# Expert weights as plain fp32 matmuls on column tiles, with two neighbouring down rows in each partition

## The chip, the cores and the metric

The kernel runs on one core of one Trainium2 chip, as one launch. A core has TensorE (PE in the profile, with the weight loads as PEld), VectorE (DVE), ScalarE (ACT), GpSimd (POOL) and SyncE (SP), which here only issues transfers, and 16 DMA engines. The metric is device time in microseconds (us). A "unit" below is 128 partitions x 2048 fp32 elements of weights, 1 MB.

## The reference, cut to what matters

Two pre-norm layers run on 256 tokens of width 1024 in fp32. Each begins with a mixer (a gated recurrence and a windowed attention side by side, merged and projected by w_o). Layer 0 has a dense SwiGLU, layer 1 has experts: each token goes to the two best of eight SwiGLU experts of inner width 3584.

```python
def moe_swiglu(h, w_router, wg, wu, wd):
    logits = (t @ w_router).astype(jnp.float32)
    top_vals, top_idx = lax.top_k(logits, TOP_K)          # TOP_K = 2 of 8
    w = jax.nn.softmax(top_vals, axis=-1)
    gates = jnp.sum(jax.nn.one_hot(top_idx, N_EXPERTS, ...) * w[..., None], axis=1)
    def expert(acc, xs):
        g_e, wg_e, wu_e, wd_e = xs                        # 1024x3584, 1024x3584, 3584x1024
        return acc + g_e[:, None] * swiglu(t, wg_e, wu_e, wd_e), None
...
for i in range(DEPTH):
    ...
    x = x + (swiglu(...) if i % 2 == 0 else moe_swiglu(h2, ...))
    gate_p = jax.nn.sigmoid(rms_norm(x, g_ple[i]) @ w_ple_gate[i])
    x = x + gate_p * (p[i] @ w_ple_up[i])
```

The last two lines are the "PLE" step; it follows the experts in layer 1 and ends the program. With the inputs of this case the router sends 69, 55, 61, 67, 62, 69, 65 and 64 tokens to experts 0 to 7.

## The kernel before

**Where the weights go.** Every weight of the program passes as units through one DMA queue, that of SP, into six `raw` slots (`load_unit`, L459). ACT copies a unit from `raw` into `w_hi`, rounded to the matmul type fp32r (L626). DVE subtracts that copy from `raw` into `w_lo`, the remainder (L984). Both have three slots. PE then makes three fp32r products for each tile of the unit: high x high and high x low of the activations (`high_products`, L1637 and L1638; in other stages L1629 and L1631), and low x high (L1644; L1630). A `raw` slot is free again, and SP may load the next unit into it, when DVE has made its `w_lo` (`low_ready`). `w_hi` and `w_lo` slots are free when PE has used the unit (`units_used`).

**The experts.** They run as items, one for each expert and up to five extra ones when an expert has more than `ROWS` = 88 tokens. Each item multiplies its 88 gathered rows (88 columns of `hT`) with one expert's weights in seven steps of 512 inner columns: two gate units, two up units, two down units each, so 42 units an item and 336 in all for eight items. One matmul of an item has 128 x 88 on one side and 512 columns of weights on the other. In a step, ACT makes the silu of the gate, DVE multiplies it with the up product, PE transposes that in four 128-column pieces (`flip`, L2103), and ACT and DVE split the result into high and low for the down product. POOL gathers the next item's rows from DRAM (`x_slots<-x_rows`, L589) and adds the finished item's rows into `x_sum` in DRAM (L583), both as indirect DMAs. The router, its `place` in each expert's list, and the first item's gather by a selection matrix stand ahead of item 0, together with the products of the PLE up projection (`ple_up_tile`). The mixer's last weights are those of w_o, whose products have the lines L1652 to L1654.

**The end.** The last item's rows are not stored but spread over the tokens by a selection matrix (`spread_piece`). DVE adds the result to x (`add_last`, L1535), PE transposes x, ACT and DVE make high and low parts of it, and then come four PLE gate units (L1629 to L1631), the sigmoid, and the output.

**What sets the order.** Each engine has its own program, written out by hand; the loops over items are `Fori` loops on every engine. Loads are issued in the order in which units are used, as slots come free.

Of the kernel before, what the change touches and what calls it, by code (L numbers as in the profile page):

```python
# [53 lines left out]
ROWS = 88  # L54
# [6 lines left out]
def build_trunk(nc, x_in, p_in, lb_logits, g_mix, w_in, q_norm, k_norm, sinks, hgrn_norm, w_pa, w_pb, w_o,  # L61
# [14 lines left out]
    EXTRA = 5  # L76
    ITEMS = EXPERTS + EXTRA + 1
    assert DEPTH == 2 and TILES == 2 and D == 1024 and HW == BANK and SW == BANK and D_FF % BANK == 0
    assert PLE == 2 * P and SEQ <= 3 * ROWS and 2 * TOP_K * SEQ < (EXTRA + 1) * (2 * ROWS + 1) and KV * 2 == 256
# [15 lines left out]
    PER_ITEM = STEPS * PER_STEP  # L95
    assert PER_ITEM % SLOTS == 0 and PER_ITEM % RAW_SLOTS == 0

# [43 lines left out]
    MOE = UP1 + 1  # L141
    MIX_AT = [MIX0, MIX1]
    END = MOE + GATE_UNITS
# [10 lines left out]
    STAGE_OF_NORM = [None, WO0_OUT, DENSE_OUT, PLE0_OUT, WO1_OUT]  # L154
    P_BANK = [4, 7]
# [9 lines left out]
    def item_down(s):  # L165
        return item_up(s + 1) + G_UNITS if s + 1 < STEPS else PER_ITEM - D_UNITS

    with ExitStack() as ctx:
# [6 lines left out]
        raw = sb("raw", [P, RAW_SLOTS, UNIT])  # L175
        w_hi = sb("w_hi", [P, SLOTS, UNIT], F32R)
        w_lo = sb("w_lo", [P, SLOTS, UNIT], F32R)
        x = sb("x", [P, TILES, D])
# [12 lines left out]
        x_slots = wide[:, 1024:2048]  # L191
        gain_rows = wide[:, 2048:3072]
        y_rows = wide[:, 3072:4096]
# [5 lines left out]
        spread = [innerT[0][:, t, P:2 * P] for t in range(TILES)]  # L199
        last_y = [[a[:, 4 * half:4 * half + 4, P:2 * P] for half in range(2)] for a in hT]  # L200
        deep = arena[:, 7680:12800]
        x_gained = deep[:, 3072:5120].rearrange("p (t n) -> p t n", t=TILES)
# [14 lines left out]
        pick = qk_mem[:, 0:256].rearrange("p (t s) -> p t s", t=TILES)  # L217
# [39 lines left out]
        logit_parts = qk_mem[0:2 * EXPERTS, 2 * SEQ:3 * SEQ]  # L257
        add_parts = sb("add_parts", [2 * EXPERTS, EXPERTS])
        pairs_mem = score_mem[:, 0:2 * TILES * EXPERTS * EXPERTS].rearrange("p (n t e f) -> p n t e f", n=2, t=TILES, e=EXPERTS)
# [10 lines left out]
        extra_of = sb("extra_of", [P, EXTRA, EXPERTS])  # L270
        second_of = sb("second_of", [P, EXTRA, EXPERTS])
        slot_columns = sb("slot_columns", [P, TILES, 2])
# [6 lines left out]
        slot_now = sb("slot_now", [P, 3])  # L279
        slot_next = sb("slot_next", [P, 3])  # L280
        slot_token = sb("slot_token", [P, 1], I32)
        sum_token = sb("sum_token", [P, 1], I32)
        pad_row = sb("pad_row", [P, 1])
        pad_now = sb("pad_now", [P, 1])
        pool_spare = sb("pool_spare", [P, 1])
        extra_expert = sb("extra_expert", [P, EXTRA])
# [12 lines left out]

        def last_act(a, part):  # L300
            return a[:, 2 * part:2 * part + 2, :].rearrange("p k (t c) -> p k t c", t=TILES)
# [9 lines left out]
        p_loaded = sem("p_loaded")  # L311
        raw_filled = [sem(f"raw{s}_filled") for s in range(RAW_SLOTS)]
# [25 lines left out]
        counted = sem("counted")  # L338
        gates_ready = sem("gates_ready")
        rows_stored = sem("rows_stored")  # L340
        slots_done = sem("slots_done")
# [5 lines left out]
        tokens_ready = sem("tokens_ready")  # L347
        spare_written = sem("spare_written")
        slot_copied = sem("slot_copied")
        slots_loaded = sem("slots_loaded")  # L350
# [57 lines left out]
        picks_ready = sem("picks_ready")  # L408
        gathered = sem("gathered")
        gatheredT_high = sem("gatheredT_high")  # L410
        gatheredT_ready = sem("gatheredT_ready")
        spread_ready = sem("spread_ready")
        slot_next_ready = sem("slot_next_ready")
        item_silu = sem("item_silu")
        item_act = sem("item_act")
        item_act_transposed = sem("item_act_transposed")
        item_actT_high = sem("item_actT_high")
        item_actT = sem("item_actT")
        item_y_done = sem("item_y_done")
        item_y_ready = sem("item_y_ready")  # L420
        last_y_high = sem("last_y_high")
        last_y_low = sem("last_y_low")
# [1813 lines left out]
```

## Time and profile before

| | |
|---|---|
| median of 3 runs | 1620.01 us (1619.46 to 1621.54) |
| profiled execution, its span | 1622.3 us |
| PE busy | 1606.5 us, 99% |
| DVE busy | 1272.1 us, 78% |
| ACT busy | 1082.4 us, 67% |
| bytes moved | 477.66 MB, mean 294 GB/s |
| the 40 slices of 40.6 us | 131 to 332 GB/s in the first 16, about 350 to 394 GB/s in the rest |

The profiled execution's only time is its span, 2.3 us above the median of the runs. Of the span, the mixers, the dense stage and layer 0's PLE fill the first 630 us, the eight items lie between about 646 and 1592 us, and the rest is the last PLE step. "Busy" of PE counts matmuls with their modelled ends, so 99% says that a matmul was nearly always in flight. A DMA share of 1 means that each of the 16 engines had a packet at all times. PEclk is the clock granted to TensorE as a share of 2.4 GHz.

### The profile page before, as it was taken

How to read it: one execution, taken by the hardware profiler on the slowest of the kernel's cores; microseconds unless marked ns; L12 is line 12 of the kernel's file. 1: busy time of each engine (PE TensorE's matmuls, PEld its weight loads, DVE VectorE, ACT ScalarE, POOL GpSimd, SP SyncE). 2: the span in 40 equal slices, each digit the busy share in tenths (PEclk: the TensorE clock that was granted, in tenths of full speed). 3: DMA queues.
4: the chain of work that ended last, by engine and by line, in shares of the span. 5: the costliest groups of instructions: out<-in, count | busy, mean ns of one | idle time of the engine just before them, and what ended most of it. 6: DMA issues, size and time to landing. Idle time of an engine off the chain costs nothing.

```text
span 1622.3 us, 22022 instructions
## 1 busy us (share of the span) xinstructions
PE 1606.5 (99%) x8472; PEld 1326.4 (82%) x8472; DVE 1272.1 (78%) x1065; ACT 1082.4 (67%) x910; POOL 103.1 (6%) x82
## 2 busy tenths in 40 slices
PE   9999999999999999999999999999999999999998
PEld 7888888888887887888888888888888888888886
DVE  7876655444578667998888888988888888889886
ACT  6665543443556656877778778778778778777774
POOL 0100000000001001050010010010010010010010
PEclk9999999999999999999999999999999999999999
DMA  9444565555464345999999999999999999999992
GB/s 332 171 157 156 185 204 181 182 197 192 159 195 148 131 156 177 393 376 379 389 380 384 393 350 388 390 377 383 389 355 386 394 363 385 386 382 383 388 370 91
DMA packets 202998, 477.66 MB, mean 294 GB/s; under 512 B 9756, under 2 KB 13436, under 8 KB 202940
## 3 DMA queue, kind: packets, MB, share of 16 engines
q1 hardware_dynamic: 198892, 465.93, 79.0%
q0 software_dynamic: 3872, 10.66, 2.5%
q8 instruction: 41, 0.67, 0.2%
q10 hardware_dynamic: 176, 0.27, 0.1%
q14 instruction: 17, 0.14, 0.0%
HBM read 469.59 MB, written 7.10 MB: 294 GB/s over the span
## 4 chain that ended last, share of the span: by engine, by line
PE 88%; DVE 4%; ACT 4%; issue 2%; DMA 2%; SPq 0%; ACTq 0%; DVEq 0%
PE ps L1637 16%; PE ps L1638 16%; PE ps L1644 16%; PE ps L1629 11%; PE ps L1631 10%; PE ps L1630 10%; ACT w_hi L626 3%; PE ps L1657 2%; DVE w_lo L984 2%; PE ps L2103 1%; PE ps L1654 1%; PE ps L1652 1%; PE ps L1653 1%; DMA raw<-in_w_moe_down 1%; PE ps L1660 1%
## 5 line engine op out<-in xcount | busy, mean ns | idle before, releaser
L984 DVE TENSOR_TENSOR w_lo<-raw,w_hi 128x2048 fp32r<-128x2048 f32 x439 | 1001.6, 2290 | 231.0 <-ACT w_hi L626 230.5
L626 ACT ACTIVATE w_hi<-raw 128x2048 fp32r<-128x2048 f32 x439 | 840.6, 1918 | 331.5 <-PE ps L1644 200.2
L1637 PE MATMUL ps<-w_hi,hT_hi 128*128 128x512 f32 x896 | 353.3, 394 | 0.0
L1638 PE MATMUL ps<-w_hi,hT_lo 128*128 128x512 f32 x896 | 349.4, 390 | 0.0
L1629 PE MATMUL ps<-w_hi,hT_hi 128*128 128x512 f32 (+1 forms) x640 | 250.6, 392 | 1.9 <-DVE w_lo L1588 1.2
L1631 PE MATMUL ps<-w_hi,hT_lo 128*128 128x512 f32 (+1 forms) x640 | 246.5, 385 | 0.0
L1630 PE MATMUL ps<-w_lo,hT_hi 128*128 128x512 f32 (+1 forms) x640 | 246.2, 385 | 0.0
L1644 PE MATMUL ps<-w_lo,hT_hi 128*128 128x512 f32 x896 | 239.7, 389 | 0.0
L1644 PEld LDWEIGHTS ps<-w_lo,hT_hi 128*128 128x128 f32 x896 | 168.2, 188 | 35.2
L1638 PEld LDWEIGHTS ps<-w_hi,hT_lo 128*128 128x128 f32 x896 | 168.4, 188 | 33.9
L1637 PEld LDWEIGHTS ps<-w_hi,hT_hi 128*128 128x128 f32 x896 | 168.2, 188 | 33.5
L1637 PE MATMUL ps<-w_hi,inner_hi 128*128 128x512 f32 x440 | 172.8, 393 | 0.8 <-DVE inner_lo L990 0.8
L1638 PE MATMUL ps<-w_hi,inner_lo 128*128 128x512 f32 x440 | 171.4, 390 | 0.0
L1629 PEld LDWEIGHTS ps<-w_hi,hT_hi 128*128 128x128 f32 x640 | 120.6, 188 | 27.2 <-issue 3.4
L1631 PEld LDWEIGHTS ps<-w_hi,hT_lo 128*128 128x128 f32 x640 | 120.5, 188 | 24.3
L1630 PEld LDWEIGHTS ps<-w_lo,hT_hi 128*128 128x128 f32 x640 | 120.7, 189 | 22.7
L1644 PE MATMUL ps<-w_lo,inner_hi 128*128 128x512 f32 x440 | 118.9, 389 | 0.0
L1637 PEld LDWEIGHTS ps<-w_hi,inner_hi 128*128 128x128 f32 x440 | 82.6, 188 | 17.9 <-ACT w_hi L626 1.2
L1644 PEld LDWEIGHTS ps<-w_lo,inner_hi 128*128 128x128 f32 x440 | 82.6, 188 | 17.4
L1638 PEld LDWEIGHTS ps<-w_hi,inner_lo 128*128 128x128 f32 x440 | 82.7, 188 | 16.8
L1629 PE MATMUL ps<-w_hi,inner_hi 128*128 128x512 f32 x151 | 59.5, 394 | 0.0
L1631 PE MATMUL ps<-w_hi,inner_lo 128*128 128x512 f32 x151 | 58.9, 390 | 0.0
(313 smaller groups left out, 1194.8 us busy)
## 6 DMA issues: line engine op xcount, KB each, us to landing
raw<-in_w_moe_gate SPq DMA_DIRECT2D x112, 1024.0 KB, 9.3
raw<-in_w_moe_up SPq DMA_DIRECT2D x112, 1024.0 KB, 9.2
raw<-in_w_moe_down SPq DMA_DIRECT2D x112, 1024.0 KB, 8.8
raw<-in_w_in SPq DMA_DIRECT2D x37, 1024.0 KB, 7.8
raw<-in_w_dense_gate SPq DMA_DIRECT2D x14, 1024.0 KB, 5.2
raw<-in_w_dense_up SPq DMA_DIRECT2D x14, 1024.0 KB
raw<-in_w_dense_down SPq DMA_DIRECT2D x14, 1024.0 KB, 4.9
raw<-in_w_o SPq DMA_DIRECT2D x8, 1024.0 KB, 4.9
```

The costliest lines, as they stand in the source:

```text
L626: nc.scalar.activation(w_hi[:, n % SLOTS, :], raw[:, n % RAW_SLOTS, :], ACT.Copy).then_inc(high_ready, 1)
L984: nc.vector.tensor_tensor(w_lo[:, n % SLOTS, :], raw[:, n % RAW_SLOTS, :], w_hi[:, n % SLOTS, :].bitcast(F32), ALU.subtract).then_inc(low_ ...
L1629: nc.tensor.matmul(o, x_parts[0][x_cols], parts[0], start=first, stop=False)
L1630: nc.tensor.matmul(o, x_parts[0][x_cols], parts[1], start=False, stop=False)
L1631: return nc.tensor.matmul(o, x_parts[1][x_cols], parts[0], start=False, stop=last)
L1637: nc.tensor.matmul(o, x_parts[0][x_cols], w, start=first, stop=False)
L1638: nc.tensor.matmul(o, x_parts[1][x_cols], w, start=False, stop=False)
L1644: return nc.tensor.matmul(o, x_parts[0][x_cols], w, start=False, stop=last)
L1652: nc.tensor.matmul(o, x_parts[0][x_cols], parts[0], start=first, stop=False)
L1653: nc.tensor.matmul(o, x_parts[0][x_cols], parts[1], start=False, stop=False)
L1654: return nc.tensor.matmul(o, x_parts[1][x_cols], parts[0], start=False, stop=last)
L1657: return nc.tensor.matmul(o, lhsT, rhs, start=start, stop=stop)
```

## The change

The change is to the expert stage and its edges. Line numbers here are those of the changed kernel.

- Expert weights are not split. PE multiplies the loaded fp32 unit as it is (L1730), and ACT and DVE no longer touch expert weights. A unit lies in one of `RING` = 14 places: five `raw` slots, a place in `arena`, the six slots of `w_hi` and `w_lo` (named `whole`), a place in `deep`, and the sixth `raw` slot. A place is free when PE has used the unit in it (`expert_units_used`).
- The array is split in column tiles. Items alternate between `BIG` (96 rows: three groups of 32 rows, four column tiles of 32 columns, 256 weight columns each) and `SMALL` (64 rows on two column tiles of 64, 512 weight columns each). The router's counts order the experts: expert 0 first, the four fullest as BIG, the others as SMALL; what does not fit becomes extra BIG items.
- Steps are 1024, 1024, 1024 and 512 inner columns wide, so 24 of an item's 42 units are gate or up units with rows of 4 KB (`128x2x1024`), four have rows of 2 KB (`128x4x512`), twelve are down units in which each partition holds two neighbouring rows, 8 KB in one piece (`128x2048`), and two are down units of 4 KB rows.
- Since neighbouring down rows share a partition, the transposes of the activations (`flip_act`, L2181) take every second column. DVE alone copies their result.
- The PLE up product is plain fp32 on column tiles, too. POOL adds an item's rows into `x_sum` as three pieces of 1 KB rows for BIG and one of 2 KB rows for SMALL.
- At the end, ACT splits PLE gate units 0 to 2 into `w_hi` ahead of taking the last item's result (`take_y`).

```diff
-ROWS = 88
+BIG = 96
+SMALL = 64
+RING = 14
...
+    def neighbour_rows(w, r0):
+        return w[r0:r0 + 2 * P, :].rearrange("(p k) n -> p k n", k=2)
...
+        ring_mem = [raw[:, (UP1 + 1 + n) % RAW_SLOTS, :] for n in range(RAW_SLOTS - 1)]
+        ring_mem += [arena[:, 12800:12800 + UNIT]]
+        ring_mem += [whole[:, part, (UP1 + n) % SLOTS, :] for part in range(2) for n in range(SLOTS)]
+        ring_mem += [deep[:, 3072:5120], raw[:, UP1 % RAW_SLOTS, :]]
...
+            def load_expert(n, source):
+                sp.dma_start(ring(n, source.shape[2]), source).then_inc(ring_filled[n % RING], 16)
+
+            for n, source in enumerate(expert_units(w_moe_gate[0, 0], w_moe_up[0, 0], w_moe_down[0, 0])):
+                if n < RAW_SLOTS - 1:
+                    sp.wait_ge(low_ready, UP1 + 1 + n - RAW_SLOTS + 1)
+                elif n == RAW_SLOTS - 1:
+                    sp.wait_ge(hgrn_out, TILES * DEPTH)
+                elif n == HI_AT:
+                    sp.wait_ge(units_used, UP1)
+                elif n == GAINED_AT:
+                    sp.wait_ge(normed_ready, TILES)
+                elif n == UP_AT:
+                    sp.wait_ge(ple_up_tiles, TILES)
+                elif n >= RING:
+                    sp.wait_ge(expert_units_used, n - RING + 1)
+                load_expert(n, source)
...
             for n, source in enumerate(PLE_UNITS[1][:GATE_UNITS]):
-                load_unit(MOE + n, source, count)
+                sp.wait_ge(expert_units_used, later_items * ITEM_UNITS + (ITEM_UNITS + n - RING + 1))
+                load_expert(n, source)
...
+                item(SMALL, final, 0)
+                for n in range(SLOTS):
+                    act_e.wait_ge(ring_filled[n], final(16 * ROUNDS, 16 * (ROUNDS + 1)))
+                    act_e.wait_ge(expert_units_used, final(ITEM_UNITS, ITEM_UNITS - RING + HI_AT + n + 1))
+                    nc.scalar.activation(w_hi[:, (UP1 + n) % SLOTS, :], ring_mem[n], ACT.Copy).then_inc(high_ready, 1)
+                take_y(SMALL, final)
...
+                def item(n_rows, at, next_rows):
+                    big = n_rows == BIG
+                    parts = BLOCKS if big else CHUNKS
+                    groups = 3 if big else 1
+                    size = 3 * D // 4 if big else D // 2
+
+                    def spans(width):
+                        n = width // len(parts)
+                        return [(part, g * n, q * n, n) for g in range(groups) for q, part in enumerate(parts)]
...
+                            weights = ring(unit, WIDTHS[s])[:, k % per, :]
+                            for part, o0, c0, n in spans(WIDTHS[s]):
+                                g = o0 // n
+                                last = mm(banks(bank, 2)[part, o0:o0 + n], item_hT[:, k, g * BLOCK:g * BLOCK + n_rows // groups],
+                                          weights[:, c0:c0 + n], k == 0 and o0 % BANK == 0, k == KD - 1, o0 % BANK > 0)
+                            if k % per == per - 1:
+                                last.then_inc(expert_units_used, 1)
```

On PE, in an item, this is what stood for a step's last gate unit and the transposes behind it (`hT_hi` and `hT_lo` are the parts of the gathered rows, `w_hi` and `w_lo` those of a unit):

```order
L1637 MATMUL ps<-w_hi,hT_hi 128x512
L1638 MATMUL ps<-w_hi,hT_lo 128x512
L1637 MATMUL ps<-w_hi,hT_hi 128x512
L1638 MATMUL ps<-w_hi,hT_lo 128x512
L1637 MATMUL ps<-w_hi,hT_hi 128x512
L1638 MATMUL ps<-w_hi,hT_lo 128x512
L1637 MATMUL ps<-w_hi,hT_hi 128x512
L1638 MATMUL ps<-w_hi,hT_lo 128x512
L1644 MATMUL ps<-w_lo,hT_hi 128x512 x4
L2103 MATMUL ps<-ident,arena 128x88 x4
```

The changed kernel has this on PE around a step's transposes, in a BIG item (24 rows of `32x256` are one unit; the first three rows are the second step's four gate units with the first step's transposes between them, the others its four up units and three down units of the first step):

```order
L1730 MATMUL ps<-whole,arena 32x256 x48
L2181 MATMUL ps<-ident,arena 128x128 x6
L1730 MATMUL ps<-whole,arena 32x256 x48
L1730 MATMUL ps<-arena 32x256 x24
L1730 MATMUL ps<-raw,arena 32x256 x24
L2161 REGISTER_ALU
L1730 MATMUL ps<-raw,arena 32x256 x120
```

And this around the same place in a SMALL item:

```order
L1730 MATMUL ps<-whole,arena 64x512 x8
L2181 MATMUL ps<-ident,arena 128x128 x4
L1730 MATMUL ps<-whole,arena 64x512 x8
L1730 MATMUL ps<-arena 64x512 x4
L1730 MATMUL ps<-raw,arena 64x512 x4
L2161 REGISTER_ALU
L1730 MATMUL ps<-raw,arena 64x512 x20
```

So a unit is twelve matmuls of 512 columns before, 24 of 256 columns on a quarter of the array in a BIG item, and four of 512 columns on half of the array in a SMALL one.

On ACT, this closed the experts before the first copies of x for the last PLE step (L860 and L864 take the last item's result, L626 splits weights, L639 is the first work on the new x):

```order
L626 ACTIVATE w_hi<-raw 128x2048
L859 REGISTER_ALU
L860 ACTIVATE hT_hi<-ps 88x4x128
L625 REGISTER_ALU
L626 ACTIVATE w_hi<-raw 128x2048
L863 REGISTER_ALU
L864 ACTIVATE hT_hi<-ps 88x4x128
L639 ACTIVATE hT_hi<-ps,params 128x256 x4
```

and this stands there now (L927 is the silu of the last item's last step, L962 splits PLE gate units, L941 takes the last item's result):

```order
L927 ACTIVATE arena<-ps 128x256
L960 ISA
L961 REGISTER_ALU
L962 ACTIVATE w_hi<-raw 128x2048
L961 REGISTER_ALU
L962 ACTIVATE w_hi<-raw 128x2048
L961 REGISTER_ALU
L962 ACTIVATE w_hi<-raw 128x2048
L934 REGISTER_ALU
L935 REGISTER_ALU
L941 ACTIVATE arena<-ps,gate_now 128x512
L744 ACTIVATE hT_hi<-ps,params 128x256 x4
```

Three splits of gate units, each waiting for its unit to land, have moved ahead of the taking of the result.

## Rows read from the trace of the kernel before

**Rows 1.** The page: engines' busy time, and GB/s in 40 equal slices
```profile
PE 1606.5 (99%) x8472; PEld 1326.4 (82%) x8472; DVE 1272.1 (78%) x1065; ACT 1082.4 (67%) x910; POOL 103.1 (6%) x82
...
GB/s 332 171 157 156 185 204 181 182 197 192 159 195 148 131 156 177 393 376 379 389 380 384 393 350 388 390 377 383 389 355 386 394 363 385 386 382 383 388 370 91
```
**Rows 2.** Busy time by window, 700 to 1500 us
```profile
core 0: us, PE busy (x) PEld busy (x) DVE busy (x) ACT busy (x) POOL busy (x), PEclk, DMA share, GB/s
700.00:1500.00 800.00, 799.39 (x3666) 659.31 (x3665) 709.54 (x453) 611.79 (x420) 58.10 (x34) 1.00 1.04 380
```
**Rows 3.** Chain of waits, 800 to 840 us: shares by line
```profile
by line: PE ps L1644 34.1%; PE ps L1637 32.6%; PE ps L1638 32.4%; PE ps L2103 1.5%
```
**Rows 4.** Waits of the SP queue, 700 to 1500 us: us, times, longest
```profile
SPq L459 <- DVE w_lo L984: 630.9, 285, 4.5
```
**Rows 5.** Groups by line and form, 700 to 1500 us: busy, mean ns | idle before, releaser
```profile
L984 DVE TENSOR_TENSOR w_lo<-raw,w_hi 128x2048 fp32r<-128x2048 f32 x286 | 652.3, 2290 | 88.3 <-ACT w_hi L626 88.0
L626 ACT ACTIVATE w_hi<-raw 128x2048 fp32r<-128x2048 f32 x286 | 547.6, 1919 | 178.3 <-PE ps L1644 173.5 <-DMA raw<-in_w_moe_gate 1.7 <-DMA raw<-in_w_moe_up 1.6
```
**Rows 6.** Timeline of PE: transposes of two steps that follow each other
```profile
814.20 0.47 PE L2103 MATMUL ps<-ident,arena 88*128 88x88 f32 x4
...
830.90 0.47 PE L2103 MATMUL ps<-ident,arena 88*128 88x88 f32 x4
```
**Rows 7.** Groups by line and form, whole span: plain fp32 matmuls
```profile
L1657 PE MATMUL ps<-arena 128*32 128x32 f32 x832 | 10.9, 199 | 3.2 <-issue 3.2
...
L1821 PE MATMUL ps<-ident,arena 128*128 128x128 f32 x48 | 6.2, 272 | 0.0
...
L1657 PE MATMUL ps<-arena,normed 128*64 128x64 f32 x96 | 4.6, 225 | 0.0
```
**Rows 8.** Timeline of PE, early stages: fp32 matmuls on column tiles
```profile
55.15 0.76 PE L1657 MATMUL ps<-arena 128*32 128x32 f32 x64
...
68.52 0.70 PE L1657 MATMUL ps<-arena 128*32 128x32 f32 x32
```
**Rows 9.** DMA issues: count, KB each, median us from issue to landing
```profile
raw<-in_w_moe_gate SPq DMA_DIRECT2D x112, 1024.0 KB, 9.3
```
**Rows 10.** Busy time by window in the experts, columns as in Rows 2
```profile
654.00:660.00 6.00, 6.00 (x28) 4.95 (x28) 4.97 (x4) 5.26 (x5) 0.06 (x1) 1.00 1.04 412
664.00:670.00 6.00, 6.00 (x28) 4.97 (x27) 5.99 (x4) 4.61 (x5) 0.00 (x0) 1.00 1.05 387
960.00:975.00 15.00, 15.00 (x70) 12.38 (x70) 13.61 (x8) 11.19 (x8) 2.84 (x1) 1.00 1.01 315
975.00:1000.00 25.00, 25.00 (x122) 20.68 (x121) 22.21 (x16) 18.87 (x15) 0.00 (x0) 1.00 1.04 396
1000.00:1010.00 10.00, 10.00 (x46) 8.29 (x45) 8.15 (x4) 9.77 (x8) 2.25 (x2) 1.00 1.06 361
```
**Rows 11.** Timeline of SP before 660 us: issues
```profile
650.92 3.67 SPq L459 DMA_DIRECT2D raw<-in_w_moe_down  x2
```
**Rows 12.** Busy time by window ahead of the first item
```profile
628.00:641.00 13.00, 11.73 (x82) 8.11 (x80) 10.49 (x32) 9.87 (x17) 1.19 (x3) 1.00 0.00 0
```
**Rows 13.** Timeline of PE: last product of w_o, first of the experts
```profile
629.01 0.40 PE L1654 MATMUL ps<-w_hi,hT_lo 128*128 128x512 f32 x1
...
646.00 0.50 PE L1637 MATMUL ps<-w_hi,hT_hi 128*128 128x512 f32 x1
```
**Rows 14.** Timeline of the end: last expert product, first adds, first gate product
```profile
1590.59 1.28 DVE L1535 TENSOR_TENSOR x<-x,ps 128x512 f32<-128x512 f32 x2 [0.95 <-PE ps L1657]
1591.94 0.39 PE L1631 MATMUL ps<-w_hi,inner_lo 128*128 128x512 f32 x1
...
1594.77 0.46 PE L1629 MATMUL ps<-w_hi,hT_hi 128*128 128x512 f32 x1
```
**Rows 15.** Busy time by window around an idle PE in layer 1's mixer
```profile
520.00:522.00 2.00, 0.00 (x0) 0.00 (x0) 2.00 (x2) 1.93 (x3) 0.00 (x0) 1.00 0.03 9
522.00:524.00 2.00, 1.54 (x17) 1.29 (x17) 2.00 (x4) 0.00 (x0) 0.00 (x0) 0.55 0.28 36
```

More of the change, by code:

```diff
@@ L311, in build_trunk @@
         p_loaded = sem("p_loaded")
+        ring_filled = [sem(f"ring{s}_filled") for s in range(RING)]
+        expert_units_used = sem("expert_units_used")
         raw_filled = [sem(f"raw{s}_filled") for s in range(RAW_SLOTS)]
@@ new lines, in take_y @@
+                def take_y(n_rows, at):
+                    act_e.wait_ge(expert_units_used, at(ITEM_UNITS, ITEM_UNITS))
+                    act_e.wait_ge(sum_rows_ready, at(1, 1))
+                    if n_rows == BIG:
+                        for g in range(3):
+                            cols = slice(g * D // 4, (g + 1) * D // 4)
+                            last = nc.scalar.activation(y_rows[:, cols], banks(0, 2)[:, cols], ACT.Copy, scale=gate_now[:, g:g + 1])
+                    else:
+                        last = nc.scalar.activation(y_rows[:, 0:BANK], banks(0), ACT.Copy, scale=gate_now[:, 0:1])
+                    last.then_inc(y_ready, 1)
@@ new lines, in experts @@
+                with act_e.Fori(0, PAIRS - 1) as t:
+                    big = lambda per, off: t * (2 * per) + off
+                    small = lambda per, off: t * (2 * per) + (per + off)
+                    item(BIG, big, SMALL)
+                    take_y(BIG, big)
+                    item(SMALL, small, BIG)
+                    take_y(SMALL, small)
+                act_e.wait_ge(routed, 1)
+                tail = act_e.value_load(n_items_i[0:1, 1:2], min_val=1, max_val=EXTRA + 1)
+                with act_e.Fori(0, tail) as t:
+                    extra = lambda per, off: t * per + (TAIL * per + off)
+                    item(BIG, extra, BIG)
+                    take_y(BIG, extra)
@@ new lines, in experts @@
+                final = lambda per, off: tail * per + (TAIL * per + off)
+                item(SMALL, final, 0)
[4 more added lines that the diff above has]
+                take_y(SMALL, final)
@@ new lines, in experts, with extra_rows @@
+                tail = dve.value_load(n_items_i[0:1, 1:2], min_val=1, max_val=EXTRA + 1)
+                with dve.Fori(0, tail) as t:
+                    def extra_rows():
+                        dve.wait_ge(small_sums, 32 + 16 * (PAIRS - 1))
+                        dve.wait_ge(big_sums, t * 48 + 48 * (PAIRS - 1))
+                        big_rows(t + TAIL)
+                        next_tokens(t + (TAIL + 1))
+                    item(BIG, lambda per, off: t * per + (TAIL * per + off), BIG, extra_rows)
@@ new lines, in experts @@
+                with pe.Fori(0, PAIRS - 1) as t:
+                    item(BIG, lambda per, off: t * (2 * per) + off, SMALL)
+                    item(SMALL, lambda per, off: t * (2 * per) + (per + off), BIG)
+                pe.wait_ge(routed, 1)
+                tail = pe.value_load(n_items_i[0:1, 1:2], min_val=1, max_val=EXTRA + 1)
+                with pe.Fori(0, tail) as t:
+                    item(BIG, lambda per, off: t * per + (TAIL * per + off), BIG)
+                item(SMALL, lambda per, off: tail * per + (TAIL * per + off), 0)
```

878 lines of the change are left out of this document (416 added, 462 removed).

## Prediction

> **What bounds the kernel now.** I read the page first: PE is busy 99% of the span, and from the 17th slice on the core moves 350 to 394 GB/s, about twice the rate of the stages before [rows 1]. So both PE and the transfers are suspects in the experts. The windows make that one number each: over 800 us of items PE is busy for 799.4 us at full clock, while the DMA share is 1.04 at 380 GB/s [rows 2]. The chain of waits there is PE alone, a third each for the three products and 1.5% for the transposes [rows 3]. Behind it stand the others: the SP queue waits 285 times for DVE's `w_lo` [rows 4], DVE and ACT spend 2.29 and 1.92 us on a unit, and ACT waits for PE [rows 5]. Nobody is waited for but PE, so what ACT and DVE do per unit is off the path and its removal alone gives nothing.
>
> PE's price of a unit: two steps' transposes start 16.70 us apart [rows 6], with six units between, 2.78 us a unit and 116.9 us an item of 42.
>
> The second reading decides this case: how much faster could the transfers go? A unit takes 9.3 us from issue to landing [rows 9], more than three times its 2.78, so the DMA queue is hardly ever empty. Two stretches in which POOL moves nothing show the rate by row length. The window around a pair of down units (4 KB rows, issued at 650.92 [rows 11]) has 412 GB/s, one of gate and up units (2 KB rows) 387 [rows 10]: 2.55 and 2.71 us for a 1 MB unit. An item before is 28 of the one and 14 of the other, 28 x 2.71 + 14 x 2.55 = 111.6 us. Once an item POOL gathers and adds, and the rate falls from 396 to 315 for 15 us and to 361 for 10 us [rows 10], a loss of 15 x 81/396 + 10 x 35/396 = 4.0 us. That is 115.6 us plus what POOL's own bytes take, and it cannot be over 116.9, since PE hardly waits. The kernel is bound by PE with the transfers about 1% behind it. Taking PE away as the bound gives almost nothing unless the transfers get faster too.
>
> **PE's new price.** The trace has plain fp32 matmuls with 32, 64 and 128 columns: 199, 225 and 272 ns [rows 7]. 32 more columns cost 26 ns, 0.81 a column; I take 0.83, two cycles at 2.4 GHz. Each fp32 matmul is two such records. On four column tiles 64 records of 32 columns end within 0.76 us, on two tiles 32 records within 0.70 [rows 8]; less the last one's 0.20 that is 35 and 31 ns for a round of one record on each tile, against 27 for the columns alone. So tiles do run side by side, with up to 8 ns a round. BIG has 24 records a k tile, six rounds of 256 x 0.83 + 8 = 221 ns: 1.33 us, 2.65 a unit. SMALL has two rounds of 433 ns, 0.87 a k tile, 1.74 a unit. The last step's narrower units cost 2.76 and 1.77. With transposes (21 and 14, and eight for the gather, at some 0.12 each by rows 6) a BIG item is 38 x 2.65 + 4 x 2.76 + 3.5 = 115 us, a SMALL one 38 x 1.74 + 4 x 1.77 + 2.6 = 76. The router's counts (69, 69, 67, 65 and 64, 62, 61, 55) fit eight items, four of each, so PE needs 764 us instead of 935. DVE's and ACT's splits go; what is left there is about 2 us a step, hidden.
>
> **The transfers' new price.** An item is 26 units of 4 KB rows, four of 2 KB and twelve of 8 KB rows. The last form is not in the trace. It may cost no less than 4 KB rows (2.55); that 4 KB rows beat 2 KB by 6% suggests somewhat less. I take 2.53, and 2.55 to 2.4 as bounds. 26 x 2.57 (408 GB/s, a little under the window's 412, which is the best of those that I saw) + 4 x 2.71 + 12 x 2.53 = 107.9 us. POOL's dips: 4.0 by the windows, at most 116.9 - 111.6 = 5.3; rows gathered fall from 88 to 80 on average, but the adds come in smaller rows. I take 5.0: 112.9 us an item, 2.69 a unit. That is under BIG's PE time by 2 us and far over SMALL's, and 14 places hold 37 us of loads, so the alternation is absorbed: PE's pair of 191 us lies behind the transfers' 226. The stage is then transfers from end to end, and its length is a sum of units.
>
> **Start.** The SP queue now has 14 places before it needs PE. Five are loaded as `raw` slots come free, as before, and the sixth behind the recurrence's output. From 628 to 641 us before, the DMA share is 0.00 [rows 12]. Units 6 to 11 wait only for w_o's last product, 629.01 [rows 13], so they fill that hole; 12 and 13 wait for x to be normalised and for the PLE up tiles, which are done by about 646, when PE begins the experts [rows 13], while six units take to 647. From 631.5 (issue and latency) the queue is never empty. POOL's copies of x and its normalised form, 3 MB, take 8 us of it, the read-back of `x_sum` 2.6. The last expert unit lands at T = 631.5 + 8 + 330 x 2.69 + 2.6 = 1530.
>
> **End.** Three PLE gate units follow in the queue and the third lands at T + 7.7. ACT must split it (1.9 [rows 5]) before it takes the last result: before, that order cost nothing; now everything behind waits. T + 9.6; taking 0.6, four fp32 spreads 1.8: T + 12. From first add to first gate product 1590.59 to 1594.77, 4.2 us, and from there 27.5 to the span's end [rows 14]: T + 43.7. PE has by then been idle for 8 us. In the mixer a PE that had been idle came back at a granted clock of 0.55, about its level of 1.2 GHz, where it was 1.00 ahead of it [rows 15]; two such windows lose 2 us. T + 45.7 = 1576. (Before: last expert product to end, 30.4 us [rows 14]; the end gets 15 us longer.)
>
> **Sum.** Span 1576 against 1622.3. The profiled time is 2.3 us above the median of the runs, so I predict 1573 for the median: eight items 4 us shorter each, some 30 us from loading ahead of PE's start, 15 lost at the end.
>
> **The rivals.**
> 1. The transfers are no faster than before, say because the 412 of one window doesn't last when 4 KB rows fill the whole stage, or POOL's smaller adds cost more. A unit at 2.78 gives T = 1560 and a median of 1604. For it: that window is 6 us long. Against: 387 and 396 are also seen with 2 KB rows in two thirds of the units. In "DMA: Bandwidth & Descriptors", "Where 436 GB/s comes from", the Trainium skill puts the limit of HBM at about 358 GB/s for a core; that would be 2.93 us a unit and about 1650, and the row of 380 GB/s over 800 us speaks against it. Chance 0.15, nearly nothing of it for the page's form.
> 2. Column tiles lose more with 256 columns than with 32. At 0.79 of ideal a BIG item is 145 us; the ring can take 37 us of loads and has six to eight units at the start, so the first BIG blocks loads for about 18 us, and later ones start with a drained ring: 1591. The Trainium skill, "TensorE: Matmul & The Clock Gate", "Measured speedup vs the span model", has 2.38x for three column tiles, which is this 0.79. The 35 ns a round of rows 8 speak against it, though with 32 columns. Chance 0.06.
> 3. Slower: only two of the four column tiles work at once at 256 columns, say for the bandwidth of the moving data. Then a BIG item is 226 us, a pair 302, PE bounds, and 646 + 4 x 302 + 30 gives 1884. It decides as soon as a pair is over 226 us plus what the end gains, that is from 150 us for a BIG item on; slower than before from about 160. Rows 8 speak against it. Chance 0.04.
> 4. Slower: TensorE's clock. In SMALL items PE waits about a third of the time, in gaps under 1 us. If it fell to its lower level for all of a SMALL item, that would be 152 us, a pair 267 and the time 1735; but at that level PE would not be idle at all, so it should come back. Chance 0.02.
> 5. The change doesn't do what it says: rounding in the router or the order gives a ninth item. 42 more units, 113 us: 1686. One expert has exactly 64 tokens. Chance 0.02.
>
> **How the numbers follow.** The forecast has 0.71. Its own range comes from POOL's dips (4.0 to 5.3), 8 KB rows (2.4 to 2.55), 4 KB rows at 412 or at 400 GB/s (26 x 0.07 = 2 us an item) and the end (2 to 5 us): 1553 to 1592. The predicted time is 1573. For 8 in 10 the range goes from 1550, a bit under it, to 1605, which takes in rival 2 and most of rival 1. This kernel's measurement can tell some 0.2% (3 us) from no change. Faster: forecast, rivals 1 and 2, 0.92; slower: 3 to 5 with something kept for a wait I have not seen, 0.07; same 0.01.
>
> **What would show it.** In the experts PE busy 80 to 88%, waiting for DMA; SP's queue no longer waits for DVE, and if for PE then hardly; GB/s above 395 outside POOL's dips; ACT and DVE under 20%; six rounds of four `32x256` records within 1.4 us; the last expert unit's first use near 1530; and in the end ACT's third split about 10 us ahead of the first add. It is wrong if PE is again busy 99% in BIG items with SP waiting for it (rivals 2 and 3), if the rate stays at 380 (rival 1), or if PEclk is below 1.0 in SMALL items (rival 4).

## The result, and the profile after

The changed kernel takes 1570.75 us (median of 4 runs, 1570.18 to 1572.23), the kernel before 1620.11 us: ratio 0.9696, 95% interval 0.9682 to 0.971, 49 us less. The forecast was 1573 us.

The page of the changed kernel, the lines that answer to [rows 1]: each engine's busy time, and GB/s in 40 equal slices.

```profile
PE 1457.7 (93%) x14692; PEld 962.8 (61%) x14692; DVE 491.4 (31%) x651; ACT 394.9 (25%) x473; POOL 72.8 (5%) x100
...
GB/s 332 189 161 146 180 192 189 181 191 186 103 262 152 141 183 178 412 405 398 358 404 402 412 398 410 401 399 404 411 387 396 414 385 403 413 386 398 414 380 34
```

The same stretch as [rows 2], busy time by window (PE, PEld, DVE, ACT, POOL; then PEclk, DMA share, GB/s):

```profile
700.00:1500.00 800.00, 713.90 (x9380) 373.74 (x9370) 48.59 (x90) 30.96 (x53) 35.71 (x46) 0.99 1.02 399
```

PE is down from 799.4 to 713.9 us of 800, DVE and ACT from over 600 to 49 and 31, and the transfers up from 380 to 399 GB/s. Three engines do much less and the time falls by 3% only: what it follows is the rate of the transfers, as the experiments show. The chain of waits over that stretch, shares by line, is now shared (compare [rows 3]):

```profile
by line: PE ps L1730 59.3%; DMA raw<-in_w_moe_down 12.2%; SPq L551 5.7%; DMA whole<-in_w_moe_gate 5.3%; DMA raw<-in_w_moe_gate 5.3%; issue 4.3%; DMA whole<-in_w_moe_up 2.6%; DMA arena<-in_w_moe_down 2.6%; PE ps L2181 1.8%; DMA whole<-in_w_m
```

PE has the largest share, though the experiments will show that it isn't the bound. When the loader waits for a free place, the chain goes back to PE's use of the unit that lay there, 14 units before, and from there along PE's own work. The SP queue does wait for PE 116 times, 261 us (waits of the SP queue, 700 to 1500 us, in the place of [rows 4]). But its units land 21.7 us after their issue (second fence, DMA issues; [rows 9] had 9.3), so that about eight units of 2.68 us are under way at a time, and the DMA share stays at 1.02:

```profile
SPq L551 <- PE ps L1730: 261.3, 116, 8.9
```

```profile
whole<-in_w_moe_gate SPq DMA_DIRECT2D x64, 1024.0 KB, 21.7
```

So here neither the chain nor the loader's waits name the bound.

Two transposes of a BIG and two of a SMALL item in PE's timeline, each pair twelve units apart, give PE's new prices:

```profile
670.42 0.98 PE L2181 MATMUL ps<-ident,arena 128*128 128x128 f32 x6
702.56 0.98 PE L2181 MATMUL ps<-ident,arena 128*128 128x128 f32 x6
...
781.60 0.74 PE L2181 MATMUL ps<-ident,arena 128*128 128x128 f32 x4
803.02 0.74 PE L2181 MATMUL ps<-ident,arena 128*128 128x128 f32 x4
```

Less the transposes' own time, (32.14 - 1.0) / 12 = 2.60 us a unit in BIG and (21.42 - 0.6) / 12 = 1.74 in SMALL. In windows without POOL's transfers (8 KB rows only, then 4 KB rows only; columns as above):

```profile
782.00:790.00 8.00, 8.00 (x39) 2.79 (x40) 0.69 (x1) 0.60 (x1) 0.00 (x0) 1.00 1.01 420
842.00:850.00 8.00, 6.08 (x29) 1.70 (x26) 0.56 (x1) 1.21 (x3) 0.00 (x0) 1.00 1.03 410
```

The window over one whole pair of items, from one gather transpose to the same one of the next pair, is 224.66 us, 112.3 an item (the window from the gather transpose at 1065.45 to the one at 1291.02 gives 112.8, the one from 1190.82 to 1413.55 gives 111.4):

```profile
966.16:1190.82 224.66, 198.20 (x2632) 104.17 (x2628) 13.32 (x24) 9.15 (x15) 9.35 (x12) 0.99 1.02 401
```

The hole of 13 us behind w_o's last product [rows 12] is closed. A short one is left ahead of it: the DMA share is 0.00 from 622 to 626 us, until w_o's last product frees the `w_hi` and `w_lo` places.

```profile
628.00:640.00 12.00, 10.89 (x106) 5.66 (x105) 6.43 (x21) 5.76 (x9) 3.51 (x6) 1.00 1.03 414
```

And the end, from the timeline of all engines, in the place of [rows 14]. L962 is the third of ACT's splits of gate units, L941 the taking of the last result:

```profile
1522.13 1.94 PE L1730 MATMUL ps<-raw,arena 128*64 128x512 f32 x8 [0.51 <-DMA raw<-in_w_moe_down]
...
1529.76 1.91 ACT L962 ACTIVATE w_hi<-raw 128x2048 fp32r<-128x2048 f32 x1 [0.59 <-DMA raw<-in_w_ple_gate]
1531.57 0.67 ACT L941 ACTIVATE arena<-ps,gate_now 128x512 f32<-128x512 f32 x1
1532.30 3.70 PE L1730 MATMUL ps<-arena 64*128 64x512 f32 x8 [8.23 <-ACT arena L941]
...
1539.27 0.79 PE L1718 MATMUL ps<-w_hi,hT_hi 128*128 128x512 f32 x1 [1.40 <-DVE hT_lo L1152]
```

PE has used the last expert unit at 1524.1 and waits 8.2 us. PEclk is 1.00 from 1523 to 1524 us and 0.60 from 1531 to 1537; the first gate matmuls start 0.43 us apart, where 0.23 is the step at the full clock later on.

### The profile page after: what moved, and what is told of

Its sections match the earlier page's. It is cut to its first block, busy times and chain, and to the rows that moved or that the text cites. A ratio compares the mean times of both kernels' runs of the same rounds, so it can differ in the third digit from the quotient of the medians.

```text
span 1568.4 us, 32592 instructions
## 1 busy us (share of the span) xinstructions
PE 1457.7 (93%) x14692; PEld 962.8 (61%) x14692; DVE 491.4 (31%) x651; ACT 394.9 (25%) x473; POOL 72.8 (5%) x100
## 4 chain that ended last, share of the span: by engine, by line
PE 74%; DMA 17%; SPq 3%; issue 3%; DVE 2%; ACT 0%; ACTq 0%
PE ps L1730 36%; PE ps L1718 11%; PE ps L1720 11%; PE ps L1719 11%; DMA raw<-in_w_moe_down 6%; SPq L551 3%; DMA whole<-in_w_moe_gate 3%; DMA raw<-in_w_moe_gate 3%; DMA whole<-in_w_moe_up 1%; DMA raw<-in_w_ple_gate 1%; DMA arena<-in_w_moe_down 1%; PE ps L2181 1%; PE ps L1727 1%; PE ps L1725 1%; PE ps L1726 1%
## 5 line engine op out<-in xcount | busy, mean ns | idle before, releaser
L1730 PE MATMUL ps<-raw,arena 128*32 128x256 f32 (+4 forms) x4320 | 335.0, 404 | 40.7 <-DMA raw<-in_w_moe_down 17.5
L1730 PE MATMUL ps<-whole,arena 128*32 128x256 f32 (+3 forms) x4480 | 334.5, 391 | 32.9 <-issue 14.2
L1730 PEld LDWEIGHTS ps<-raw,arena 128*32 128x32 f32 (+1 forms) x4320 | 164.5, 115 | 207.8 <-issue 88.0
L1730 PEld LDWEIGHTS ps<-whole,arena 128*32 128x32 f32 (+1 forms) x4480 | 172.7, 115 | 172.5 <-issue 77.5
L1068 DVE TENSOR_TENSOR w_lo<-raw,w_hi 128x2048 fp32r<-128x2048 f32 x99 | 226.1, 2290 | 125.4 <-ACT w_hi L728 125.2
L728 ACT ACTIVATE w_hi<-raw 128x2048 fp32r<-128x2048 f32 x99 | 189.2, 1914 | 111.1 <-PE ps L1720 105.4
L927 ACT ACTIVATE arena<-ps 128x768 f32<-128x768 f32 (+3 forms) x32 | 20.4, 637 | 662.3 <-PE ps L1730 662.3
L1730 PE MATMUL ps<-arena 128*32 128x256 f32 (+7 forms) x2600 | 142.9, 314 | 21.0 <-ACT arena L941 8.2
L1718 PEld LDWEIGHTS ps<-w_hi,hT_hi 128*128 128x128 f32 x640 | 120.6, 189 | 28.7 <-issue 2.6
L1720 PEld LDWEIGHTS ps<-w_hi,hT_lo 128*128 128x128 f32 x640 | 120.6, 188 | 24.5
L1719 PEld LDWEIGHTS ps<-w_lo,hT_hi 128*128 128x128 f32 x640 | 120.8, 189 | 22.5
L1730 PEld LDWEIGHTS ps<-arena 128*32 128x32 f32 (+4 forms) x2600 | 81.6, 117 | 77.4 <-issue 33.0
L1718 PE MATMUL ps<-w_hi,inner_hi 128*128 128x512 f32 x136 | 53.2, 391 | 0.0
L1720 PE MATMUL ps<-w_hi,inner_lo 128*128 128x512 f32 x136 | 53.0, 390 | 0.0
## 6 DMA issues: line engine op xcount, KB each, us to landing
whole<-in_w_moe_gate SPq DMA_DIRECT2D x64, 1024.0 KB, 21.7
```

Source lines behind the costliest of these rows:

```text
L728: nc.scalar.activation(w_hi[:, n % SLOTS, :], raw[:, n % RAW_SLOTS, :], ACT.Copy).then_inc(high_ready, 1)
L927: nc.scalar.activation(item_act[:, 0:taken], banks(GATE, 2)[:, 0:taken], ACT.Silu).then_inc(silu_ready, 1)
L1068: nc.vector.tensor_tensor(w_lo[:, n % SLOTS, :], raw[:, n % RAW_SLOTS, :], w_hi[:, n % SLOTS, :].bitcast(F32), ALU.subtract).then_inc(low_ ...
L1718: nc.tensor.matmul(o, x_parts[0][x_cols], parts[0], start=first, stop=False)
L1719: nc.tensor.matmul(o, x_parts[0][x_cols], parts[1], start=False, stop=False)
L1720: return nc.tensor.matmul(o, x_parts[1][x_cols], parts[0], start=False, stop=last)
```

## Experiments

Nine kernels, all timed against the kernel before in 3 rounds, the sixth in 5. Theory A: the expert stage is now a sum of transfers. Theory B: the gain comes from PE's shorter work.

### One part undone: down rows of 4 KB

```diff
-                return [neighbour_rows(down, s * D + c0) for c0 in range(0, D, 2 * P)]
+                return [rows(down, (s * D + c0) // P, UNIT // D) for c0 in range(0, D, 2 * P)]
...
-                            last = nc.tensor.transpose(banks(TRA, 2)[:, cols], of_unit[:, c % 2, :] if WIDTHS[s] == D else item_act[:, cols],
+                            last = nc.tensor.transpose(banks(TRA, 2)[:, cols], item_act[:, cols],
```

> The changed kernel with one part undone: the twelve down units of an item come as two separate rows of 4 KB in each partition instead of two neighbouring rows, 8 KB in one piece, and the transposes take contiguous columns. Theory A (the expert stage is a sum of transfers from end to end): in the profile after, windows with only 8 KB rows show about 424 GB/s and those with only 4 KB rows 410, so a down unit goes from 2.47 to 2.56 us, 12 x 0.085 = 1.0 us an item, 8 us in all: 1579. Theory B (the gain comes from PE, and transfers lie hidden behind it): 1571, since PE's work is the same.

Measured: 1577.05 us (1575.53 to 1578.57), ratio 0.974 (0.9723 to 0.9756). 6.3 us more than the changed kernel, 0.066 us for each of 96 down units, where 8 us were expected. PE's work is the same, so theory B is out for this part.

### The other row length: gate and up in pieces of 2 KB

```diff
         def columns_of(w, s):
             per = UNIT // WIDTHS[s]
+            if per == 2:
+                return [rows(w, k0, 4)[:, :, s * D + c0:s * D + c0 + BANK] for k0 in range(0, KD, 4) for c0 in (0, BANK)]
```

> The changed kernel with gate and up units loaded in pieces of 2 KB as before (4 x 512 columns a partition) instead of 4 KB (2 x 1024); the products use the places as if they held the wide form, so the part of the computation that changes is the order of the weights in the gate and up products. Theory A: 24 units an item go from 2.56 us (410 GB/s) to 2.72 (385 GB/s), 3.9 us an item, 31 in all: 1602. Theory B: 1571.

Measured: 1592.84 us (1592.43 to 1594.12, 3 runs), ratio 0.9834 (0.9815 to 0.9854). (A fourth run took 3490 us, which no run of another kernel here did; why is not known, it is left out, and nothing is built on it.) 22.1 us more, 0.115 us for each of 192 units instead of the 0.16 that I had expected. Theory A in kind, about 70% of it in size.

### Both

The two edits together.

> Both of the former together: the changed kernel with the row lengths of the kernel before, 2 KB for gate and up, 4 KB for down (the gate and up products use wrongly ordered weights). Theory A: 8 + 31 = 39 us more than the changed kernel, 1610, so that plain fp32 on column tiles with 14 places is worth only some 10 us by itself, out of loads ahead of PE's start and less what the end costs. Theory B: 1571.

Measured: 1600.26 us (1597.99 to 1600.77), ratio 0.9877 (0.986 to 0.9893). 29.5 us over the changed kernel, against 6.3 + 22.1 = 28.4 from the two alone, so they add (39 had been expected, of which 31 for the 2 KB rows). The same window as above, 700 to 1500 us:

```profile
700.00:1500.00 800.00, 699.13 (x9284) 359.60 (x9274) 46.84 (x84) 30.36 (x52) 35.75 (x46) 0.99 1.04 386
```

PE is less busy than in the changed kernel and the kernel slower. Against the kernel before, plain fp32 on column tiles with 14 places and the new end is worth 19 us, the row lengths 29.5.

This run also gives both prices of the kernel before at the same row lengths. PE's gather transposes of two items that follow each other, in the kernel before, and those of one pair to the next, in this run:

```profile
875.94 0.77 PE L2167 MATMUL ps<-ident,arena 88*128 88x88 f32 x8
993.84 0.77 PE L2167 MATMUL ps<-ident,arena 88*128 88x88 f32 x8
```

```profile
971.92 0.88 PE L2226 MATMUL ps<-ident,arena 96*128 96x96 f32 x8
1205.22 0.88 PE L2226 MATMUL ps<-ident,arena 96*128 96x96 f32 x8
```

An item took PE 117.9 us before, and takes the transfers 233.30 / 2 = 116.6 us with the same row lengths.

### The row lengths alone, in the kernel before

```diff
+    def long_units(gate, up, down):
+        units = []
+        for s in range(STEPS):
+            c0 = s // 2 * D if s < 6 else D_FF - D
+            for w in (gate, up):
+                units += [rows(w, (4 * s + 2 * u) % KD, 2)[:, :, c0:c0 + D] for u in range(2)]
+            if s:
+                units += [neighbour(down, s - 1, u) for u in range(2)]
+        return units + [neighbour(down, STEPS - 1, u) for u in range(2)]
...
-            for n, source in enumerate(mixer_units(w_moe_gate[0, 0], w_moe_up[0, 0], w_moe_down[0, 0])):
+            for n, source in enumerate(long_units(w_moe_gate[0, 0], w_moe_up[0, 0], w_moe_down[0, 0])):
```

> The kernel before (split weights, three products) with the expert units loaded in the row lengths of the changed kernel: 4 KB pieces for gate and up, 8 KB for down (products use wrongly ordered weights). If PE bounds the kernel before, as its chain of waits says, the time stays at 1618 to 1621, and what changes is only how early units land: issue to landing falls from 9.3 us to about 5. If the transfers were the bound before already, it falls by 39 us to about 1581.

Measured: 1619.47 us (1618.88 to 1621.92), ratio 1.0001 (0.9991 to 1.001). No change that can be measured. The units land earlier, 7.3 us after their issue where [rows 9] has 9.3 (about 5 had been expected), only to wait for PE, which is as busy as before. The DMA issues (count, KB, median us to landing), then the window:

```profile
raw<-in_w_moe_gate SPq DMA_DIRECT2D x112, 1024.0 KB, 7.3
```

```profile
700.00:1500.00 800.00, 799.38 (x3665) 659.13 (x3664) 709.06 (x451) 611.73 (x420) 56.36 (x32) 1.00 1.00 380
```

So the row lengths are worth 29.5 us in one kernel and 0 in the other: before, PE stood a hair ahead of the transfers. The change had to move both.

### Loads ahead of PE's start

```diff
                 elif n == HI_AT:
-                    sp.wait_ge(units_used, UP1)
+                    sp.wait_ge(second_hT_ready, 1)
```

> The changed kernel, but the seventh expert unit (and so all behind it) waits until the first item's gathered rows are ready, about 15 us later than w_o's last product, for which it waits now. It tells what the loads ahead of PE's start are worth. Theory A: in the profile after the queue is always full from 627 us; 15 to 17 us without expert loads are lost except for the 8 us in which POOL's copies of x run, which now move into the hole, so 7 to 10 us more: 1579. Rival: PE's spare time makes up for a late start, and the time stays at 1571.

Measured: 1581.87 us (1581.39 to 1582.46), ratio 0.9763 (0.9749 to 0.9778), 11.1 us more than the changed kernel, a little over the 7 to 10 expected. The window from 630 to 640 us has 83 GB/s in place of 414:

```profile
630.00:640.00 10.00, 10.00 (x101) 5.38 (x99) 4.91 (x18) 3.59 (x5) 3.52 (x6) 1.00 0.21 83
```

PE is as busy there, and from 700 to 1500 us it has 11% of its time to spare (708.5 us busy); it can't make up for units that have not been moved.

### The end in another order

```diff
                 item(SMALL, final, 0)
-                for n in range(SLOTS):
-                    act_e.wait_ge(ring_filled[n], final(16 * ROUNDS, 16 * (ROUNDS + 1)))
-                    act_e.wait_ge(expert_units_used, final(ITEM_UNITS, ITEM_UNITS - RING + HI_AT + n + 1))
-                    nc.scalar.activation(w_hi[:, (UP1 + n) % SLOTS, :], ring_mem[n], ACT.Copy).then_inc(high_ready, 1)
                 take_y(SMALL, final)
+                gate_high(tail, range(0, 1))
...
                     high(range(0, 4))
+                    between()
                     act_e.wait_ge(item_added, 4)
...
                 add_last(2)
+                gate_low(range(0, 1))
                 norm_low(5, PLE_GAIN + KD, range(0, 2))
                 add_last(3)
                 norm_low(5, PLE_GAIN + KD, range(2, 4))
+                gate_low(range(1, SLOTS))
```

Here `gate_high` and `gate_low` are the loops that stood ahead of `take_y` on ACT and ahead of the adds on DVE, and `between` makes the high parts of units 1 and 2.

> The changed kernel with another order at the end: ACT takes the last item's result first and splits PLE gate unit 0 behind it, units 1 and 2 behind the first four copies of x; DVE adds before it makes the low parts. In the profile after, the last expert product ends at 1524.1 and the result is taken at 1531.6, behind the third split. If that order is what costs, the first gate product comes 7 to 8 us earlier: 1563. Rival: the gate units' landing and splitting is itself the path (the third lands 7.7 us behind the last expert unit), so that only the wait moves: 1569 to 1571.

Measured: 1561.94 us (1560.59 to 1562.67, 5 runs), ratio to the kernel before 0.9639 (0.9626 to 0.9652): 8.8 us under the changed kernel, and the fastest kernel here that leaves nothing out. Its timeline at the same place:

```profile
1521.90 1.94 PE L1738 MATMUL ps<-raw,arena 128*64 128x512 f32 x8 [0.52 <-DMA raw<-in_w_moe_down]
1523.97 0.69 ACT L942 ACTIVATE arena<-ps,gate_now 128x512 f32<-128x512 f32 x1 [19.47 <-PE ps L1738]
...
1524.71 1.99 PE L1738 MATMUL ps<-arena 64*128 64x512 f32 x8 [0.87 <-ACT arena L942]
...
1531.06 0.79 PE L1726 MATMUL ps<-w_hi,hT_hi 128*128 128x512 f32 x1 [2.49 <-DVE hT_lo L1156]
```

The last expert unit arrives at the same time; the result is taken 7.6 us earlier and the first gate product comes 8.2 earlier. The spreads take 1.99 us in place of 3.70: behind 0.87 us of waiting PEclk is 1.00 (1524.5 to 1526.7 us), behind 8.23 us in the changed kernel it was 0.60 (1531 to 1537 us).

### POOL's share of the transfers

```diff
-                    nc.gpsimd.indirect_dma_start(out=x_slots[0:rows_of, :], out_offset=None, in_=x_rows[:, :],
-                                                 in_offset=bass.IndirectOffsetOnAxis(slot_token[0:rows_of, 0:1], 0)).then_inc(slots_loaded, 16)
+                    nc.gpsimd.indirect_dma_start(out=x_slots[0:2, :], out_offset=None, in_=x_rows[:, :],
+                                                 in_offset=bass.IndirectOffsetOnAxis(slot_token[0:2, 0:1], 0)).then_inc(slots_loaded, 16)
...
-                                                     out_offset=bass.IndirectOffsetOnAxis(sum_rows[:, g:g + 1], 0),
-                                                     in_=y_rows[:, g * D // 4:(g + 1) * D // 4], in_offset=None,
+                                                     out_offset=bass.IndirectOffsetOnAxis(sum_rows[0:2, g:g + 1], 0),
+                                                     in_=y_rows[0:2, g * D // 4:(g + 1) * D // 4], in_offset=None,
```

and the same for SMALL's add.

> The changed kernel, but POOL's indirect transfers in the items move two rows each instead of 64 to 128 (left out: the other rows' gathers and adds, so the items' inputs and sums are not those of the reference). Theory A with POOL's dips: in a pair of items of the profile after the queue of the weights loses about 8.5 us of 225 in the stretches in which POOL's packets run, 4.2 an item; with seven gathers and seven adds gone that is some 29 us: 1542. Rival: the dips come from something else (code fetches of PE, its stalls), then 1565 or more.

Measured: 1545.84 us (1545.2 to 1548.31), ratio 0.9545 (0.953 to 0.956): 24.9 us under the changed kernel (29 had been expected), 3.6 us for each of the seven items whose rows POOL gathers and adds. The same pair of items, now 217.93 us instead of 224.66:

```profile
960.53:1178.46 217.93, 199.02 (x2632) 104.57 (x2628) 13.32 (x24) 9.14 (x15) 8.29 (x12) 0.98 1.02 408
```

That is 3.4 us an item; the next pairs differ by more (from the transposes at 1178.46 to 1390.24, 211.78 us against 222.73). So most of what an item loses in the dips, 3.4 us or somewhat more, comes from POOL's rows.

### More work for PE

```diff
                             for part, o0, c0, n in spans(WIDTHS[s]):
                                 g = o0 // n
+                                if bank == GATE and not big:
+                                    mm(banks(bank, 2)[part, o0:o0 + n], item_hT[:, k, g * BLOCK:g * BLOCK + n_rows // groups],
+                                       weights[:, c0:c0 + n], k == 0 and o0 % BANK == 0, False, o0 % BANK > 0)
...
-                                          weights[:, c0:c0 + n], k == 0 and o0 % BANK == 0, k == KD - 1, o0 % BANK > 0)
+                                          weights[:, c0:c0 + n], k == 0 and o0 % BANK == 0 and (big or bank != GATE), k == KD - 1,
+                                          o0 % BANK > 0)
```

> The changed kernel, but in SMALL items each gate matmul is made twice (the gate product is doubled, so silu's input is not the reference's). PE gets 14 units x 1.74 = 24 us more in each of four items. Theory A: a pair then needs 207 to 215 us of PE, still under the 225 of its transfers: 1571 to 1573. Theory B (PE, busy for 89% of the stage, is on the path): up to 97 us more, 1668.

Measured: 1571.75 us (1570.52 to 1573.24), ratio 0.9699 (0.9684 to 0.9714), 1.0 us more than the changed kernel, within its uncertainty.

```profile
700.00:1500.00 800.00, 776.09 (x9808) 436.97 (x9798) 47.54 (x85) 30.92 (x53) 35.68 (x46) 1.00 1.02 398
```

PE goes from 713.9 to 776.1 us of 800 and GB/s stay at 398. So theory B is out for the whole stage: PE is 97% busy and off the path.

### Half of the places

```diff
-RING = 14
+RING = 7
...
-        ring_mem += [deep[:, 3072:5120], raw[:, UP1 % RAW_SLOTS, :]]
+        ring_mem = ring_mem[0:RING]
...
-                elif n == GAINED_AT:
-                    sp.wait_ge(normed_ready, TILES)
-                elif n == UP_AT:
-                    sp.wait_ge(ple_up_tiles, TILES)
...
-                    act_e.wait_ge(expert_units_used, final(ITEM_UNITS, ITEM_UNITS - RING + HI_AT + n + 1))
+                    act_e.wait_ge(expert_units_used, final(ITEM_UNITS, ITEM_UNITS))
```

and the same last change for DVE's low parts: the splits of the gate units now wait for the use of the last expert unit.

> The changed kernel with 7 places for expert units instead of 14 (the first seven of the same list; the end as in the changed kernel). Theory A with the ring as cover: seven places hold 18 us of loads instead of 36. At the start the queue runs dry until PE frees a place at about 648, of which POOL's 8 us of copies use a part, as in the late start, 11 us; and PE's own stops (twice 4.7 us at the turn of its loop over pairs, 1.5 and 2.5 us late in the first BIG item) and the BIG items, whose 113 us of PE stand against 112.5 of transfers, are covered less, 2 to 4 us a pair: 1571 + 11 + 8 to 16, 1590 to 1598. Rival: PE is fast enough that the depth beyond six or seven does nothing after the start: 1582.

Measured: 1597.17 us (1594.32 to 1598.33), ratio 0.9853 (0.9835 to 0.9871), 26.4 us more. The window 628 to 640 us, then the stage:

```profile
628.00:640.00 12.00, 10.89 (x106) 5.67 (x105) 6.42 (x20) 6.30 (x10) 3.47 (x6) 1.00 0.30 118
...
700.00:1500.00 800.00, 702.86 (x9305) 358.89 (x9296) 46.84 (x84) 30.32 (x52) 35.68 (x46) 0.99 1.02 392
```

The late start cost 11.1 us by itself, so some 15 are left for the stage, as expected (8 to 16). 392 against 399 GB/s over the stage's 890 us is 16 us, too. The changed waits at the end have little part in it: from the last expert unit's first use to the end of the span it is 47.7 us (1548.84 to 1596.5), 46.3 in the changed kernel and 47.5 in the first experiment, whose end is untouched. Depth is part of the gain, and not only for the start. Which part of the 15 is PE's stops and which a thinner queue (a window without POOL's transfers, 1100 to 1150 us, has 405 GB/s against the changed kernel's 411) was not taken apart.

## Why the prediction was right

**The bound before.** It rested on two prices 1% apart: PE 116.9 us an item and transfers 115.6 and more [rows 6, 9, 10]. The row lengths in the kernel before gave 0 us, in the changed kernel 29.5: that is what such a pair must show. Both prices were about 1 us too low. PE's was 42 units at the mean of six, without the item's gather transposes and the rest of its edge, and came to 117.9; the transfers' came to 116.6, which with 111.6 for the units leaves 5.0 for the dips. So the 116.9 that served as the transfers' upper bound was not one, but the distance between the two was about 1%, as forecast.

**PE's new price.** 2.65 us a BIG unit was forecast, 2.60 measured; 1.74 for SMALL, 1.74 measured. The four tiles do run side by side at 256 columns: 2.60 us is twelve rounds of 216 ns, 9 ns over one record's 207 ns of columns, close to the 8 ns taken from rounds of 32 columns [rows 8]. The Trainium skill, "TensorE: Matmul & The Clock Gate", "Measured speedup vs the span model", has 2.38x on three column tiles; four tiles here come to about 2.60 us where the columns alone, at 0.81 ns, would be 12 x 207 ns = 2.49, 4% less. The trace does not show a loss like that at this shape.

**The transfers' new price.** 112.9 us an item was forecast (its units add up to 108.0, not 107.9, which changes nothing), 111.4 to 112.8 measured. Its terms: 4 KB rows 408 GB/s assumed, 410 seen. 8 KB rows 2.53 us a unit assumed, 1048.6 KB at 420 GB/s is 2.50. POOL's dips 5.0 us assumed; moving few rows took away 3.4 to 3.6 of it, by the time and by the first pair. The limit of about 358 GB/s for a core in "DMA: Bandwidth & Descriptors" of the Trainium skill, "Where 436 GB/s comes from", does not hold here: 399 over 800 us were measured, with the program on one core.

**The start.** The stream was to begin at 631.5 and began at 627.3; the last unit's first use was to be 1530 and was 1522.1. For one half of these 8 us there is a plain cause: the profiled execution of the kernel before had a stop of PE ahead of [rows 15], 3.2 us and a half-clock stretch behind it, which the changed kernel's does not have. Waits of PE, 500 to 560 us, of the changed kernel and then of the kernel before with longer rows, whose mixer is untouched:

```profile
PE ps L1730 <- issue: 0.7, 1, 0.7
```

```profile
PE ps L1671 <- issue: 0.6, 1, 0.6
```

So the stop belongs to that execution and not to the program: w_o's last product came at 624.97, where the kernel before had it at 629.01, and it came at 624.97 in the kernel before with longer rows, too. That is also why that execution's span, 1622.3, stood above the median of the runs; the span of the kernel with longer rows, 1618.5, lies 1.8 below the time of the same run. The forecast took its 2.3 off and so took most of the stop out again. The span was 7.6 us shorter than forecast (1568.4 against 1576), the median only 2.3 (1570.75 against 1573). The other half of the 8 us is the 0.01 us a unit by which 2.69 was too high, over 330 units.

**The end.** T + 45.7 was forecast, T + 46.3 measured. The working had PE idle for 8 us behind the three splits and 2 us more lost to the clock; the rows have 8.23 and, in the spreads, 1.7, and another order gave back 8.8.

**What was off.** Three of the signs came out otherwise. PE was busy 89% of the stage where 80 to 88 had been named. The SP queue waited for PE 261 of 800 us where "hardly" had been named, and the first add was said to be 10 us behind ACT's third split, where the working's own terms have 4.3 and the rows 4.7 (1529.76 to 1534.47). In the expectations the 2 KB rows were charged with 0.16 us a unit, and 0.115 was measured; 385 GB/s was read from the changed kernel's last steps, where POOL's gather runs beside the only units with 2 KB rows. In the prediction's price of the changed kernel only four units of an item have 2 KB rows, so this hardly enters.

The forecast's last sum, eight items 4 us shorter each, 30 us from loads ahead of PE's start and 15 lost at the end, had its total right and two terms off that cancelled. By the rows, 330 units from 627.3 to 1522.1 less POOL's 10.6 are 112.5 us an item, 5.4 less than 117.9, so the items gave 43 us and not 32. The end got 16 us longer (46.3 against 30.4). The spans of 1618.5 and 1568.4 then leave 23 us for the loads ahead, not 30.

The gain of 49 us, as the experiments give it: the row lengths are 29.5 us, and 19.3 to 19.9 is left for the rest. That rest holds about 10 from the items (116.6 against 117.9 us, eight times) and 11.1 from loads ahead of PE's start, and is less by the 8.8 that the end's order costs. These make 12. The other 7 no run took apart; the late start, for one, left the first six units loaded ahead of PE as they were.

## What to carry to other kernels

- Where two resources are within a few per cent of each other, price both for every edit. PE's work on an item fell by about a fifth (117.9 us to a mean of 94 by its prices a unit) and the time by 3%, because the transfers were next; and the transfer edit that gave 29.5 us here gave nothing with PE in front.
- When a stream of weights is the bound, every microsecond in which the queue is empty counts, at its start too, and engine time counts for nothing until it comes near the stream's. Rows of 8 and 4 KB in place of 4 and 2 KB were worth about 3 and 4% of a unit here.
- At this program's end the order on ACT, which waits for transfers, was on the path, 8.8 us: put what is ready first.

## What the hardware showed that I had not expected

PE stopped for 4.7 us twice, each time at the turn of its loop over pairs, with nothing in the profile to wait for, and behind the first it came back at half clock (fp32 rounds 0.43 us apart instead of 0.22, PEclk 0.83 from 850 to 860 us). With shorter stops, 11 of them and most in the narrow last step of a BIG item, where 2.5 us come back in all four, the waits of PE over the stage have 28.4 us for which the profile shows no cause:

```profile
PE ps L1730 <- issue: 28.4, 13, 4.7
```

The kernel before had none of that length in its expert stage (the longest wait of PE there, 646 to 1588 us, is 0.8 us, for DVE). The page of the profile counts 118 packets on the instruction queue in place of 41; that the stops are fetches is a guess that no run here tested. The transfers went on through the first one, with a DMA share of 1.04 from 850 to 860 us, and the changed kernel's time did not follow PE. In a kernel bound by PE they would presumably be paid in full.
